# Input projections without attention in one Strassen stage with a bitwise key search; index scores in column groups; one out projection

## What is computed

```python
x = x + 0.5 * g1 * swiglu(h, w_ffn1_in, w_ffn1_out)
h = modulate(rmsnorm(x, norm_mix), sh2, sc2)
q, k, v, qi, ki, wi, z, xbc, dt_raw, gate_a, gate_s = split(h @ w_in)
att   = attend(q, k, v, qi, ki, wi)           # keys chosen by the index scores
ssd_y = ssd_branch(z, xbc, dt_raw, ...)       # conv, silu, scan, skip, gate, norm
merged = sigmoid(gate_a) * (att @ w_attn_out) + sigmoid(gate_s) * (ssd_y @ w_ssd_out)
x = x + g2 * (merged @ w_out)
x = x + 0.5 * g3 * swiglu(modulate(rmsnorm(x)), w_ffn2_in, w_ffn2_out)
```

## Time and profile before

| what | us |
|---|---|
| three runs: lowest, median, highest | 4562.23, 4564.63, 4566.98 |
| the profiled execution, its own time | 4567.95 |
| its span, first to last instruction | 4566.2 |
| feed-forward f1 (75.8 to 938) | 862.2 |
| index scores (1237 to 1374) | 137.0 |
| SSD branch without time steps (1396.3 to 2745) | 1348.7 |
| gates and gathering (2774 to 3060) | 286.0 |
| attention (3060 to 3361) | 301.0 |

### The profile page before, as it was taken

How to read it: one execution, slowest core, us unless ns; L and a number is a source line. 1 busy time by engine, 2 the same in 40 slices (tenths; PEclk the granted TensorE clock), 3 DMA queues, 4 the chain that set the end, 5 groups by cost and what they waited for, 6 DMA issues and landing times. The chain is left out here.

```text
span 4566.2 us, 47951 instructions
## 1 busy us (share of the span) xinstructions
PE 4077.6 (89%) x17644; PEld 2978.1 (65%) x17644; DVE 2345.6 (51%) x3956; ACT 764.7 (17%) x1512; POOL 292.7 (6%) x325
## 2 busy tenths in 40 slices
PE   6999999969897979979879877988999879999997
PEld 4888888846564646645646644654546558888885
DVE  3444444420038878879789785304453044444444
ACT  2111111121021201201201200015620021111111
POOL 0000000000000200200200200305400000000000
PEclk8999999989968979979979978989998989999999
DMA  4333333241331011011011011220021212222221
GB/s 178 111 138 120 120 122 113 80 195 60 95 56 39 16 55 41 11 57 39 13 55 39 15 53 54 85 93 20 10 70 60 74 55 92 84 81 95 83 86 72
DMA packets 105162, 335.20 MB, mean 73 GB/s; under 512 B 18632, under 2 KB 54736, under 8 KB 86464
## 3 DMA queue, kind: packets, MB, share of 16 engines
q1 hardware_dynamic: 89984, 280.03, 18.2%
q10 hardware_dynamic: 11808, 31.85, 1.9%
q0 software_dynamic: 3200, 21.11, 1.3%
HBM read 289.56 MB, written 43.56 MB: 73 GB/s over the span
## 5 line engine op out<-in xcount | busy, mean ns | idle before, releaser
L737 PE MATMUL banks<-h,arena 128*128 128x344 f32 x1920 | 567.7, 459 | 36.5 <-DMA arena<-in_w_ssd 36.5
L737 PEld LDWEIGHTS banks<-h,arena 128*128 128x128 f32 x1920 | 370.7, 193 | 233.7 <-issue 47.9
L572 ACT ACTIVATE f_u<-f_Y 128x258 f32<-128x258 f32 x408 | 157.7, 387 | 1101.2 <-PE f_Y L510 1101.2
L737 PE MATMUL banks<-y,arena 128*128 128x344 f32 x768 | 239.3, 474 | 38.0 <-DVE y L1938 30.2
L653 DVE TENSOR_TENSOR f_g<-f_u,f_Z 128x258 f32<-128x258 f32 x136 | 57.7, 424 | 390.8 <-PE f_Z L510 390.8
L2122 PE MATMUL gg_ps<-h,gg_w 128*128 128x344 f32 x768 | 234.8, 470 | 9.8 <-DMA gg_w<-in_w_g 9.2
L737 PE MATMUL pja_ps<-h,pja_w 128*128 128x344 f32 x720 | 211.1, 457 | 27.3 <-DMA pja_w<-in_w_att 27.3
L737 PEld LDWEIGHTS banks<-y,arena 128*128 128x128 f32 x768 | 151.7, 199 | 125.6 <-issue 35.7
L2122 PEld LDWEIGHTS gg_ps<-h,gg_w 128*128 128x128 f32 x768 | 151.7, 199 | 90.8 <-DMA gg_w<-in_w_g 10.0
L623 DVE TENSOR_TENSOR f_g<-f_u,f_X 128x258 f32<-128x258 f32 x136 | 57.6, 424 | 292.8 <-PE f_X L510 292.5
L737 PEld LDWEIGHTS pja_ps<-h,pja_w 128*128 128x128 f32 x720 | 138.2, 192 | 100.2 <-issue 29.9
(11 more groups left out here) (354 smaller groups left out, 6814.6 us busy)
## 6 DMA issues: line engine op xcount, KB each, us to landing
raw<-in_w_f1i SPq DMA_DIRECT2D x44, 1024.0 KB, 4.8
raw<-in_w_f2i SPq DMA_DIRECT2D x44, 1024.0 KB, 4.7
f_wa<-in_w_ada SPq DMA_DIRECT2D x14, 2048.0 KB, 9.6
arena<-in_w_ssd SPq DMA_DIRECT2D x40, 512.0 KB, 3.6
raw<-in_w_f1o SPq DMA_DIRECT2D x16, 1024.0 KB, 4.7
raw<-in_w_f2o SPq DMA_DIRECT2D x16, 1024.0 KB, 4.8
n_w<-in_w_ada SPq DMA_DIRECT2D x4, 2048.0 KB, 19.9
scr_kidx<-pja_pages POOLq DMA_DIRECT2D x4, 2048.0 KB, 7.7
```

The lines of the kernel that those rows point to most:

```text
L572: nc.scalar.activation(u[:, i % 2, n], bank[i % 2][:, 0:SUB], ACT.Copy).then_inc(done, 1)
L737: m = nc.tensor.matmul(ps[q][:, c, 0:NC], slots[:, q, k], rhs[:, k, c * NC:(c + 1) * NC], start=k == 0, stop=k == kt - 1)
```

## The change

1. `index_scores` forms two prompt heads at a time and keeps four relu results. For the samples it loads the keys of four samples at once, forms the dots of all four side by side in groups of 32 of PE's columns, 512 key columns per matmul, and weighs them by 64 matmuls of 8 columns. The scores stay in SBUF as `sc2`, 128 partitions x 2 x 129, and no longer go through DRAM.
2. `top_round` and its helpers go. The 256th highest score of each row is found by fixing its 32 bits one after the other: VectorE counts the scores at or above a candidate, PE sums the samples' counts over partitions (`vote`), VectorE decides the bit.
3. A stage `dense` takes the place of the four `ssd_project` and of the 16 gate tiles: 28 pairs of tiles (12 of x, 8 of z, 4 of each gate) in the Strassen scheme, 56 half-steps in all, with the search's bits, convolutions, activations and the final choice between. Its results go to DRAM (`xc`, `z`, `gs`, `ga`).
4. The loops over groups and chunks are written out. `ssd_scan` loads each chunk from DRAM by SP in place of ACT's copy, and then x and z for the gate; `ssd_post` takes the place of `ssd_out`, without projection and search. The groups' results stay in `h` and `S`.
5. `project_and_gather` takes the place of `gate_and_gather`: 8 tiles of one out projection over all 16 input tiles, 384 matmuls, each product multiplied by its gate from DRAM; after each tile the one-hot matmuls and gathers of one sample.
6. `attend` turns three chunks ahead and then weighs two and turns two. `time_steps` no longer clears `S`. The layout of the weights follows.

The diff, cut to its core:

```diff
 def index_scores(nc, d, scr, pj, tok, ident, mask, sc2):
...
+            def dot(f, q):
+                n = f * QUADS + q
+                if n >= 2:
+                    pe.wait_ge(rectified, UP + n - 1)
+                for j in range(HALFB):
+                    pe.wait_ge(k_in[j], UP + 32 * (f + 1))
+                    nc.tensor.matmul(pD[n % 2][COL * j:COL * (j + 1)], qx[:, :, f * HALFB + j],
+                                     kx[:, j, 4 * q:4 * q + 4].rearrange("p i s -> p (i s)"), start=True, stop=True).then_inc(dots[j], 1)
...
+            for n in range(len(PAIRED)):
+                prompt(n)
+                if n == 3:
+                    pe.wait_ge(weighed, UP + 1)
+                if n >= 4 and n % 2 == 0 and done < 2 * QUADS:
+                    dot(done // QUADS, done % QUADS)
+                    if done:
+                        weigh((done - 1) // QUADS, (done - 1) % QUADS)
+                    done += 1
...
+def dense(nc, d, o, scr, h, flat, mask, sc2, blk, cw, cb, smc, cnt, seln, page_pos, ident):
...
+            for p in range(M):
+                if p + RING < M:
+                    sp.wait_ge(p3, UP + 2 * p + 2)
+                    sp.wait_ge(p4, UP + 2 * p + 2)
+                    sp.wait_ge(made_s, UP + 4 * p + 4)
+                    sp.dma_start(raw[:, p % RING], d["w_dense"][p + RING]).then_inc(w_in[p % RING], 16)
...
+            for i in range(N + 1):
+                if i < N:
+                    if i % 2 == 0:
+                        pe.wait_ge(w_in[i // 2 % RING], UP + 16 * (i // 2 // RING + 1))
+                    if i >= 2:
+                        pe.wait_ge(yread, UP + i - 1)
+                    product(i, left(i, 0), "11", Y, True, p1)
...
+                    product(i, total(i)[:, 2], "t3", Y, False, p7)
+                vote(i)
...
+            def counts(j, ns):
+                for n in ns:
+                    scratch, done = (pre, eq)[n % 2], (nb + 2) * j + n
+                    if done >= 2:
+                        dve.wait_ge(counted, UP + done - 1)
+                    src = rows[n] if n < nb else sc2[:, n - nb]
+                    nc.vector.tensor_scalar(scratch[:, 0:src.shape[1]], src, thr(n), None, ALU.is_ge, ALU.add,
+                                            accum_out=count[:, n:n + 1]).then_inc(counted, 1)
...
+            for i in range(N + 1):
+                if i >= 1:
+                    half(i - 1)
+                if 1 <= i <= BITS:
+                    decide(i - 1)
+                if i < BITS:
+                    counts(i, range(3))
+                if i < N:
+                    first(i)
+                if i < BITS:
+                    counts(i, range(3, nb + 2))
+                if i % 2 and i // 2 + 1 < M:
+                    pair_sums(i // 2 + 1)
+                if i >= 1:
+                    rest(i - 1)
+                if i >= 2 and i // 2 - 1 in rank:
+                    convolve(i // 2 - 1, i % 2)
...
-                nc.scalar.activation(st[:, s], xc[:, :, bass.ds(c * P, P)], ACT.Copy).then_inc(staged, 1)
...
+            for c in range(TB):
+                if c >= 2:
+                    sp.wait_ge(yoff, UP + c - 1)
+                sp.dma_start(st[:, c % 2], xc[:, :, c * P:(c + 1) * P]).then_inc(staged[c % 2], 16)
+            if first is not None:
+                first(sp)
             sp.wait_ge(h2, UP + TB + 1)
             sp.dma_start(o["ssm_p"][g], hT[:]).then_inc(saved, 16)
...
+        for g in range(SG):
+            y = (h, S)[g // 2][:, 4 * (g % 2):4 * (g % 2) + 4]
...
+            ssd_scan(nc, arena, banks, o, g, scr["xc"][g], y, dt, dtA, ea, te, etot, upper, below, ident, hT, skip_and_gate)
+            ssd_sample(nc, arena, banks, d, o, g, smc[:, g * XT:(g + 1) * XT], y, dt, dtA, dskip, ones, ident, kept)
+            ssd_post(nc, arena, banks, SH // SG // 2 * NB * DS, kept, g, xz, xz_in, y, ones, dskip, nssd)
...
+            for t in range(KT):
+                pe.wait_ge(w_in[t % 2], UP + 16 * (t // 2 + 1))
                 for c in range(NCH):
...
+                    for k in range(KD):
+                        m = nc.tensor.matmul(ps[n % BANKS][:, 0:NC], w[:, t % 2, k], rhs(k, c), start=k == 0, stop=k == KD - 1)
+                    m.then_inc(pmm, 1)
```

More of the change, by code:

```diff
@@ L904, in _, with prompt @@
-            sp.wait_ge(stored, UP + 32)
+                    sp.dma_start(kx[half * ID:(half + 1) * ID, j], src).then_inc(k_in[j], 16)
         @block.tensor
         def _(pe):
-            pe.wait_ge(small, UP + 80)
+            def prompt(n):
+                b, t = PAIRED[n]
+                W = (b + 1) * P
+                for u in range(2):
+                    if n:
+                        pe.wait_ge(relu, UP + 2 * (n - 1) + u + 1)
+                    for c in range(0, W, 512):
+                        e = min(c + 512, W)
+                        m = nc.tensor.matmul(ps[:, u, c:e], pj[64 * u:64 * u + ID, QI0 + t, b * P:(b + 1) * P],
+                                             pj[64 * u:64 * u + ID, KI0, c:e], start=True, stop=True)
+                    m.then_inc(mm[u], 1)
@@ L916, in sample @@
[L916 to L936, removed]
@@ L937, in _ @@
-            for b in range(len(CHOSEN), NB):
-                sample(b)
-            pe.wait_ge(summed, UP + NB)
+            nc.tensor.matmul(pG, wl[:].rearrange("k j c -> k (j c)"), wpick, start=True, stop=True).then_inc(newd, 1)
+            done = 0
+            for n in range(len(PAIRED)):
[7 more added lines that the diff above has]
+                    done += 1
@@ L940, in _ @@
+            weigh(1, QUADS - 1)
+            pe.wait_ge(placed, UP + 1)
+            for c in range(2):
+                nc.tensor.matmul(pL[:, c:c + 1], place[:, c], snew[:], start=True, stop=True)
+            pe.wait_ge(placed, UP + 3)
             for c in range(2):
@@ L945, in _, with rectify @@
         def _(act):
[L946 to L953, removed]
+            def rectify(n):
+                for j in range(HALFB):
+                    act.wait_ge(dots[j], UP + n + 1)
+                nc.scalar.activation(rl[:, n // QUADS, n % QUADS].rearrange("p i s -> p (i s)"), pD[n % 2][:], ACT.Relu).then_inc(rectified, 1)
+            done = 0
+            for n, (b, t) in enumerate(PAIRED):
+                for u in range(2):
+                    hd = 2 * n + u
+                    act.wait_ge(mm[u], UP + n + 1)
+                    if hd >= 4:
+                        act.wait_ge(acc, UP + hd - 3)
+                    nc.scalar.activation(r[:, hd % 4, 0:(b + 1) * P], ps[:, u, 0:(b + 1) * P], ACT.Relu).then_inc(relu, 1)
+                if n >= 4 and n % 2 == 0 and done < 2 * QUADS:
+                    rectify(done)
+                    done += 1
         @block.gpsimd
@@ L1614, in ssd_scan @@
+def ssd_scan(nc, arena, banks, o, g, xc, y, dt, dtA, ea, te, etot, upper, below, ident, hT, first=None):
     R, PD = SH // SG, DI // SH
@@ L1637, in turns, with half @@
         def turns(eng, turn):
-            with eng.Fori(0, TB // 2 - 1) as i:
-                for s in range(2):
-                    turn(2 * i + s, s)
+            for c in range(TB - 2):
+                turn(c, c % 2)
+        def half(c, s):
+            return (c - s) // 2
         @block.gpsimd
@@ L1940, in _ @@
[L1940 to L1948 removed]
+            nc.vector.reciprocal(rstd[:], rstd[:]).then_inc(inv, 1)
@@ L1951, in final_norm @@
+            dve.wait_ge(inv, UP + 1)
+            for t in range(GT):
+                nc.vector.scalar_tensor_tensor(out=y[:, t], in0=y[:, t], scalar=nssd[:, g * GT + t:g * GT + t + 1],
+                                               in1=rstd[:], op0=ALU.mult, op1=ALU.mult).then_inc(scaled, 1)
+            dve.wait_ge(scaled, UP + GT)
 def final_norm(nc, o, x, y, ones, gain_d):
@@ L2149, in _ @@
+                if b >= 2:
+                    pe.wait_ge(read, UP + b - 1)
+                pe.wait_ge(hotd, UP + NPAGE * (b + 1))
+                for p in range(NPAGE):
+                    for f in range(2):
+                        m = nc.tensor.matmul(pE[b % 2][f][:, 0:3], hots[:, p, f * P:(f + 1) * P], vals[:, b * NPAGE + p],
+                                             start=p == 0, stop=p == NPAGE - 1)
+                m.then_inc(used, 1)
         @block.vector
```

874 lines of the change are left out of this document (505 added, 369 removed).

## The result

The changed kernel takes 4425.95 us (median of 4 runs, 4422.52 to 4428.56) against 4565.41 of the kernel before (4 runs, 4562.23 to 4566.98): a ratio of 0.9695, with a 95% interval of 0.9678 to 0.9712. That is 139 us less. The forecast was 73 less, in a range whose low end, 4430, lies 4 us above the result. The sign was right and the size was half. The profiled execution took 4425.19 us, its span is 4423.4.

What follows compares the result with a forecast made beforehand. The prediction saw TensorE busy 89% of the span and VectorE 51%. Branch -69, gather +5, index scores -5, attention -5 and time steps +1 sum to -73 us: 4492 on the median's scale, range 4430 to 4600.

Steps and rivals of the forecast that it cites:

- Dense: New projection stage: 56 half-steps at 12.18 us, 682, plus votes 14, search stalls 5 and rims 24.5, sum 726 us.
- The vote: Dense stage, PE: 32 votes at 0.45 us each with a wait, 14 us in all (bounds 8 and 32).
- The counts: Dense stage, VectorE: the search's comparisons that also count, 5.9 us for 4482 columns (bounds 3.3 and 6.5).
- (b): Dense stage: VectorE bounds it if counts cost twice the estimate; about 4645, with half that excess about 4570; chance 0.08.
- (c): Dense stage: Strassen saving not kept, late votes, slots and stores stretch steps by 1.3 us; about 4565; chance 0.10.
- Scan and groups: SSD branch: chunk loads stall 1.4 us for each of 6 chunks; scan 74 us, group 138.5, four groups 554.
- Rival (a): Scan: a transfer wait in each chunk lets the clock sink; 144 us more, about 4635; chance 0.11.
- The gather stage: Gate tiles swapped for out tiles with the same 384 matmuls, 0; cold weights and late gathers, +5 (-8 to +20).
- my +5: Gather stage: cold weights and the last sample's late gathers, against 20 us of PE idle, +5 us (-8 to +20).
- Index scores: Index scores: 47.8 us of sample matmuls become 20, plus two key waits of 8 and 16: -5 (-25 to +10).
- Attention and time steps: Attention: turns in batches, -5 us (-12 to +10); time steps: +1 us.
- Rival (d): Better case: no scan stall (-50 over four groups), index scores at full clock (-20); about 4425; chance 0.15.

Runs made afterwards that it cites:

- runs 5 and 6: Changed kernel with an eighth product in 52 of dense's 56 steps, 4511.51 us; changed kernel without the key search's 32 bit rounds, 4423.59 us.
- Run 4: Changed kernel with each scan chunk's load issued later, behind the diagonal product of two chunks before instead of its state product: 4544.80 us.
- Run 1: Kernel before, with only TensorE's loop over sample pairs in the gather stage written out: 4535.49 us, ratio 0.9933.
- run 7: Changed kernel with room for seven samples' index keys instead of four, relu results in a ring of two: 4410.85 us, ratio 0.9662.

## Why the prediction was right and wrong

**Dense: right, 10 us too dear.** The step of 12.18 us from the feed-forward part held, at a clock of 1.00, and TensorE bounded it (runs 5 and 6). The vote was mis-sized: 0.23 us a step, not 0.45, so 7 us; the other 2 or 3 lie in the stalls and the rims. The counts, bounded from far rows, came out at 5.9 us a step, from 1716.80 to 1722.95 in one of them with 0.25 for what stands between, as I had taken. Rivals (b) and (c) are out: the step is 12.4, and VectorE's waits on TensorE's path are 3 us in all.

**Scan and groups: right mechanism, 21 us too dear.** The stall is there and ends on the DMA, as forecast, but it makes a chunk 1.05 us longer, not 1.4. The load takes 3.4 us where I took 3.7 from the row of 512 KB. A group is 133.1 us, not 138.5: the scan 3.4 less, of which the stalls are 6 x 0.35 = 2.1, sample and post together 2.

**Rival (a) did not happen.** Run 4 shows it with a wait 2.7 us longer, with 2.5 to 6 us at a clock of 0.50 behind each wait of 3.5; waits between the two lengths were not tried.

**The gather stage: the step that failed.** "The 16 gate tiles leave (counted above as PE's 227 us) and 8 out tiles of 48 matmuls come, the same 384 matmuls: 0", and the stage set against its "20 us of PE idle today". By the prediction's own sign of being wrong, "if the stages that I moved by 5 move by 20", this is where it failed. The sum took all the busy time as fixed, and left out the busy time of the one-hot matmuls. It fell by 17 us; the groups by line, before and after:

```profile
L2142 PE MATMUL gg_pE<-gg_vals,gg_hots 128*128 x512 | 31.5, 171 | 0.3
```

```profile
L2371 PE MATMUL gg_pE<-gg_vals,gg_hots 128*128 128x3 f16 x512 | 14.1, 164 | 0.0
```

That stage's four bursts of 8 us, and the clock of 0.50 to 0.53 in the 3.4 us behind each, went because a loop was written out, an edit that I had read as one of the branch's form and priced at nothing. Run 1 gives the old kernel the whole 27 us by that alone. Against that written-out old stage the new projection with its late gathers costs +3, close to my +5.

**Index scores: the right sign for another reason.** I set 20 us of new matmuls and 24 of waits against 47.8. Measured: dots 21.6, weighings 9.3 and waits 15.8, 46.7 in all, against 48.6 with the 0.8 of waits before, so the samples' part gave 2. The gain is the prompt's dots, 14.4 us shorter for the same 160 records, as the stage's clock rose from 0.59 to 0.71. Their mean length goes with the stage's clock in four executions: 845 ns at 0.59 before, 736 at 0.65 in run 4, 673 at 0.71 in the changed kernel, 622 at 0.80 in run 7. I had priced every matmul that stayed at its old duration. Why the clock rose is not shown: TensorE had more gaps there than before, busy for 85 of 122.5 us against 117 of 137. What left the stage are 256 matmuls of 16 columns, and no run puts them back alone.

**Attention and time steps** were right within 3 us.

Rival (d) had priced 4425 by "No stall in the scan" and "scores at the full clock". The result meets that number, but the scan did stall and the scores stand at a clock of 0.71: the number was hit without its reason. The range ended 4 us too high because its good end took in the good ends of scan and scores alone, and the gather stage's own, -8, was far from the -25 it gave.

## What to carry to other kernels

Price the loop form as an edit of its own; here it was worth 27 us. Where a change writes a hardware loop out, look in the trace for short instructions that take an operand by the loop's counter, and compare them with the same instruction written out, as the one-hot matmuls here with 63 ns in the old loop and 26 without it. I had priced the work that the change leaves alone in a stage at a clock of 0.59 at its old duration, and the prompt's dots fell from 845 to 673 ns there as the stage's clock came to 0.71: give such work a range. Where a copy within the chip becomes a load behind the same event, try one more buffer at once; here it gave 28 us back.

## What the runs showed of the hardware

One-hot matmuls of three columns took 25 to 27 ns each written out, 52 to 56 in a loop within the changed kernel at a clock of 1.00, and 63 in the loop of the kernel before, where the mean clock of the burst shown is 0.78. In the first scan of the changed kernel six chunks with a wait of 0.82 to 0.95 us each stood at a clock of 1.00; in run 4, behind waits of 3.5 to 3.65 us, the next 2.5 to 6 us stood at 0.50. A comparison that also sums its result took VectorE 1.27 us for 1024 columns in float32, and a multiplication by one scalar, without the sum, 0.75.
